# Norm chains at stage changes: work by halves of rows, two ones products a norm, a shared last scaling

## What is computed

```python
def rms_norm(x, w):
    xf = x.astype(jnp.float32)
    y = xf * lax.rsqrt(jnp.mean(xf * xf, axis=-1, keepdims=True) + EPS)
    return (y * w.astype(jnp.float32)).astype(x.dtype)

for layer in range(DEPTH):                       # first block, DEPTH = 2
    mix = mixer(rms_norm(h, norm_pre))
    h = h + rms_norm(mix, norm_post)
    ff = squared_relu_mlp(rms_norm(h, mlp_norm_pre[layer]), mlp_w_up[layer], mlp_w_down[layer])
    h = h + rms_norm(ff, mlp_norm_post[layer])
...
x = x + merged @ w_out[i]                        # second block
x = x + cross_attention(rmsnorm(x, norm_cross[i]), rmsnorm(mem, norm_mem[i]), ...)
x = x + jnp.square(jax.nn.relu(rmsnorm(x, norm_ffn[i]) @ w_up[i])) @ w_down[i]
return rmsnorm(x, norm_final)
```

## Time and profile before

| | |
|---|---|
| median of 3 runs | 2653.78 us (2652.63 to 2654.26) |
| the profiled execution | 2652.97 us, of which the profile's span is 2651.2 us |
| PE busy in the span | 2552.5 us, 96% |
| DVE, ACT, POOL busy | 55%, 44%, 5% |
| PE's share of the chain that ended last | 76% |

### The profile page before, as it was taken

The page is one execution under the profiler, slowest core; times in us unless marked ns, Lnnn a source line. Parts: engine busy times, 40 slices in busy tenths (PEclk is TensorE's granted clock), DMA queues, the critical chain, the costliest instruction groups (busy, mean ns, idle before and its releaser), DMA issues.

```text
span 2651.2 us, 31918 instructions
## 1 busy us (share of the span) xinstructions
PE 2552.5 (96%) x12498; PEld 2076.4 (78%) x12498; DVE 1469.3 (55%) x2349; ACT 1156.8 (44%) x2068; POOL 145.7 (5%) x144
## 2 busy tenths in 40 slices
PE   7999999999999999999989999999999999999998
PEld 5888778878676678888877888878877787788886
DVE  5555454334466654344367888787476566453343
ACT  4254443223356645233246665666245444442232
POOL 1110010000010000000000010000000010000000
PEclk9999999999999999999989999999999999999999
DMA  4212123662232222322323212222321243233222
GB/s 132 72 56 64 61 75 103 125 139 96 80 98 74 79 64 88 103 96 88 103 60 95 63 58 64 64 64 72 104 66 51 71 143 104 72 102 97 96 95 72
DMA packets 188598, 226.00 MB, mean 85 GB/s; under 512 B 8416, under 2 KB 121344, under 8 KB 188192
## 3 DMA queue, kind: packets, MB, share of 16 engines
q1 hardware_dynamic: 188448, 223.95, 28.0%
HBM read 213.96 MB, written 9.44 MB: 84 GB/s over the span
## 4 chain that ended last, share of the span: by engine, by line
PE 76%; DVE 14%; ACT 6%; issue 3%; DMA 2%; POOL 0%; SPq 0%; DVEq 0%; POOLq 0%; ACTq 0%
PE bank L1778 20%; PE bank L1780 20%; PE bank L1779 20%; DVE CV L2473 3%; DVE wlo L2249 2%; PE bank L1784 2%; PE bank L1796 2%; PE bank L1785 2%; PE bank L1786 2%; PE bank L1813 1%; DMA raw<-in_down 1%; DVE E L2522 1%; ACT whi L2032 1%; PE bank L1964 1%; PE bank L1972 1%
## 5 line engine op out<-in xcount | busy, mean ns | idle before, releaser
L2249 DVE TENSOR_TENSOR wlo<-raw,whi 128x1024 fp32r<-128x1024 f32 (+1 forms) x389 | 489.4, 1263 | 719.1 <-ACT whi L2032 717.0
L2032 ACT ACTIVATE whi<-raw 128x1024 fp32r<-128x1024 f32 (+1 forms) x389 | 408.7, 1057 | 647.9 <-PE bank L1780 592.2
L1778 PE MATMUL bank<-XAh,whi 128*128 128x512 f32 x1536 | 615.6, 401 | 19.4 <-DVE XAl L2257 10.9
L1780 PE MATMUL bank<-XAh,wlo 128*128 128x512 f32 x1536 | 602.3, 392 | 0.0
L1779 PE MATMUL bank<-XAl,whi 128*128 128x512 f32 x1536 | 602.2, 392 | 0.0
L1778 PEld LDWEIGHTS bank<-XAh,whi 128*128 128x128 f32 x1536 | 290.7, 189 | 97.8 <-issue 32.2
L1780 PEld LDWEIGHTS bank<-XAh,wlo 128*128 128x128 f32 x1536 | 290.6, 189 | 62.2
L1779 PEld LDWEIGHTS bank<-XAl,whi 128*128 128x128 f32 x1536 | 291.2, 190 | 58.7 <-issue 0.7
L1778 PE MATMUL bank<-XBh,whi 128*128 128x512 f32 x816 | 324.5, 398 | 2.9 <-DVE XBl L2255 1.7
L1780 PE MATMUL bank<-XBh,wlo 128*128 128x512 f32 x816 | 318.0, 390 | 0.0
L1779 PE MATMUL bank<-XBl,whi 128*128 128x512 f32 x816 | 317.9, 390 | 0.0
(11 more groups left out here) (328 smaller groups left out, 3423.4 us busy)
## 6 DMA issues: line engine op xcount, KB each, us to landing
raw<-in_w_in SPq DMA_DIRECT2D x76, 512.0 KB, 3.7
raw<-in_up SPq DMA_DIRECT2D x64, 512.0 KB, 3.5
raw<-in_down SPq DMA_DIRECT2D x64, 512.0 KB, 3.7
raw<-in_a_w_in SPq DMA_DIRECT2D x32, 512.0 KB, 4.0
raw<-in_w_up SPq DMA_DIRECT2D x32, 512.0 KB, 3.6
raw<-in_w_down SPq DMA_DIRECT2D x32, 512.0 KB, 3.6
raw<-in_w_kv SPq DMA_DIRECT2D x16, 512.0 KB, 3.6
raw<-in_w_ssd_branch SPq DMA_DIRECT2D x16, 512.0 KB, 3.4
```

Source lines behind the costliest of these rows:

```text
L1778: pe.matmul(out, wh[:, w, c], xh[:, x, 0:s.ntok], start=st, stop=False)
L1780: m = pe.matmul(out, wl[:, w, c], xh[:, x, 0:s.ntok], start=False, stop=en)
L2032: act.activation(s.hi, s.raw, ACT.Copy).then_inc(s.whi[0], 1)
L2249: dve.tensor_tensor(s.lo, s.raw, s.hi.bitcast(F32), ALU.subtract).then_inc(s.wlo[0], 1)
```

## The change

- `ones` has two products instead of three: tile 6's square is added to the sum too, always on DVE (`left=1`, "sq_add_v"); only tile 7's square is apart.
- Where a norm closes a stage (the four changes and the end), tile 7 leaves its bank in two halves of 256 rows; square, ones products (each half in a bank of its own), logarithm and exponential follow by halves. Tile 0 is scaled, added and split by halves as well.
- Scaling and adding to `h` are two steps now, `res_scale` and `residual`, both on DVE, and the addition of tile k stands behind the split of tile k - 1. (A table could put some additions on POOL; it is empty.)
- The mixers' output products and the last quarter of every `down` product end with tiles 6 and 7 in units of their own.
- While the first tile is prepared, PE gets two products of constants (`WARM`, ones x `cst`), whose result nobody reads.
- A unit that isn't its product's last goes X tile by X tile: all outputs for tile 0, then all for tile 1.
- Behind the second MLP the squares for `norm_mix_2` are taken tile by tile with the splits (`early=True`), and their sums go to POOL instead of DVE.
- At the end ACT multiplies tiles 1 and 4 of `h` by the gain once they are squared; after the factor POOL multiplies these two by `r`, and DVE does the other six.

```diff
-NRAW, NW = 3, 3
+NRAW, NW, WARM = 3, 3, 2
+ADD_ON_POOL = ()
+BY_POOL = 1, 4
...
-            if i < nk - 2:
-                st["added"] = add(by, t=st["sum"], q=q, sq=sq, before=st["added"], n=n, added=sig("sq.add")).added
+            if i < nk - left:
+                st["added"] = add(by if i < nk - 2 else "sq_add_v", t=st["sum"], q=q, sq=sq, before=st["added"], n=n, added=sig("sq.add")).added
...
+            for b, (c0, m) in zip(banks, parts):
+                t = add("ones", q=st["sum"], sq=st["added"], bank=b, c0=c0, n=m, first=True, final=False, ones=sig("ones")).ones
...
+    HALVES = slice(0, 256), slice(256, S)
...
+            if k == 7:
+                es = mix_halves(mx[:, k, :], bk, m, list(mx_free), plus)
+                mt[k] = es[1]
+                bk.free(es[1])
+                tile.halves([mx[:, k, c] for c in HALVES], es)
...
                 if k < 8:
-                    a = add("residual", mx=mx[:, k, :], mix=mt[k], gain=col(g + k), r=r, rfin=rt, h=h[:, k, :], h_ready=ht[k], res=sig("res"))
-                    ht[k] = a.res
+                    sc_ = [add("res_scale", mx=mx[:, k, c], mix=mt[k], gain=col(g + k), r=r.t[:, c], rfin=f, scaled=sig("res.scaled")).scaled
+                           for c, f in (parts if k == 0 else [(ALL, rt[1])])]
                 if k > 0:
                     yield k - 1
+                if k < 8:
+                    halves_of_h[k] = [add("residual_pool" if k in ADD_ON_POOL else "residual", ...).res
+                                      for c, v in zip(HALVES if k == 0 else [ALL], sc_)]
...
+        b = ring_all.take()
         for k in tiles:
+            if k == 0:
+                b.free(add("warm", bank=b, n=WARM, warm=sig("warm")).warm)
             nxt(k)
...
-        p.run(out_gemm_a(6, 2))
+        p.run(out_gemm_a(6, 1))
+        p.run(out_gemm_a(7, 1))
...
-                for hf in range(2):
+                for k0, n in ((0, 4), (4, 4)) if qt < 3 else ((0, 4), (4, 2), (6, 1), (7, 1)):
...
-    nxt, squares, ones = into(XB, "norm_mix_2", "sq_add_v")
+    nxt, squares, ones = into(XB, "norm_mix_2", early=True)
...
+            if s.ends:
+                turns = [(n, o, kk) for n, o in enumerate(s.outs) for kk in range(s.nk)]
+            else:
+                turns = [(n, o, kk) for kk in range(s.nk) for n, o in enumerate(s.outs)]
...
+        elif k == "pre_gain":
+            act.activation(s.h, s.h, ACT.Copy, scale=s.gain).then_inc(s.gained[0], 1)
...
+        if s.kind == "final_pool":
+            pool.tensor_tensor(s.h, s.h, s.r.t[:, :], ALU.mult).then_inc(s.scaled[0], 1)
```

More of the change, by code:

```diff
@@ L446, in rms_close @@
         r = rrs.take()
+        if isinstance(b, list):
+            f = [add("rfin", bank=b[x], ones=m, r=r, c0=x * 256, n=256, dim=dim, rfin=sig("rfin")).rfin for x, m in enumerate(ones)]
+            for x in range(2):
+                b[x].free(f[x])
+            return r, f
         f = add("rfin", bank=b, ones=ones, r=r, n=n, dim=dim, rfin=sig("rfin"))
@@ L487, in rms_steps, with mix_halves @@
         return r, rt
+    HALVES = slice(0, 256), slice(256, S)
+    def mix_halves(mx, bk, m, mx_free, plus):
+        return [add("mix", mx=mx[:, c], bank=bk, cols=c, unit=m, mx_free=mx_free, plus=plus, mix=sig("mix")).mix for c in HALVES]
+    halves_of_h = {}
     def post_norm(mx, g):
@@ L513, in gained, with gained_halves, into @@
         split(X, k, h[:, k, :], ht[k], scale=col(g + k))
-    def into(X, g, by="sq_add"):
-        tile, ones = norm_sum(8, by=by)
+    def gained_halves(X, k, g):
+        for c, v in zip(HALVES, halves_of_h[k]):
+            X.ready[k] = sig("xlo")
+            add("xsplit", hi=X.hi[:, k, c], lo=X.lo[:, k, c], src=h[:, k, c], src_ready=v, src2=NONE, scale=col(g + k), x_free=X.after, xhi=sig("xhi"), xlo=X.ready[k])
+    def into(X, g, by="sq_add", left=1, early=False):
+        tile, ones = norm_sum(8, by=by, left=left)
         def nxt(k):
@@ L521, in nxt @@
                 X.open()
-            gained(X, k, gain[g])
+            (gained_halves if k == 0 and 0 in halves_of_h else gained)(X, k, gain[g])
+            halves_of_h.clear()
+            if early:
+                tile(hsrc(k), ht[k])
         def squares():
             for k in range(8):
-                tile(hsrc(k), ht[k])
+                if not early:
+                    tile(hsrc(k), ht[k])
                 yield
@@ L868, in evac @@
                         yield
[L869 removed]
+                    yield from gemm(us[qt % 2], 8, down, [(k0 * P, n * P)], [("fm", x * P) for x in range(n)], evac, k0=qt * 8, ring=ring_all)
             XB.open()
@@ L1795, in pe_program @@
                 on.room(s.bank)
-            pe.matmul(s.bank.t[:, 0:s.n], K.ones, s.q.t[:, 0:s.n], start=s.first, stop=s.final).then_inc(s.ones[0], 1)
+            c = slice(s.get("c0", 0), s.get("c0", 0) + s.n)
+            pe.matmul(s.bank.t[:, c], K.ones, s.q.t[:, c], start=s.first, stop=s.final).then_inc(s.ones[0], 1)
+        elif k == "warm":
+            on.wait_ge(*K.cst_in)
+            on.room(s.bank)
+            for _ in range(s.n):
+                m = pe.matmul(s.bank.t[:, :], K.ones, K.cst[:, 0:512], start=True, stop=True)
+            m.then_inc(s.warm[0], 1)
         elif k == "hg_diag":
```

128 lines of the change are left out of this document (84 added, 44 removed).

## The result

The changed kernel takes 2645.55 us (median of 8 runs, 2640.93 to 2647.72) where the kernel before takes 2653.89 us on the same chip (8 runs): ratio 0.9967, 95% interval 0.9958 to 0.9976. That is 8.3 us or 0.33% faster, where I had predicted 19.7 us; 2645.5 lies outside my range of 2625 to 2644. Run again beside other kernels it took 2643.65 (4 runs); the median of all twelve is 2645.4.

What follows compares the result with a forecast made beforehand. TensorE, busy 2552.5 of 2651.2 us, was taken as the bound, with idle time, extra norm products and half clock to win. Terms 6.4 + 4.5 + 4.2 + 4.0 + 0.6 = 19.7 us gave 2633.3, 2634 against the median; range 2625 to 2644.

Steps and rivals of the forecast that it cites:

- 1, the chain by halves: At changes one to three, halves of tiles bring PE's first product sooner: 1.7, 3.0 and 1.7 us, 6.4 in all.
- 2, the clock: At changes one to three, shorter idle time keeps PE's clock up more: 1.5 us each, 4.5 in all.
- 12 products of tile 0 give 2.7 us, and DVE's next tile comes 2.05 us later, 2.25 with the new order: At the first change, the order by X tiles removes PE's 0.34 us wait for X tile 1.
- my gap of 2.3 us: Idle time left ahead of PE's first new product; assumed clock loss 1.1 us at each change.
- the change does little: Rival: PE's start is bound by something else, as the next unit's weight split; 2644 to 2652 us, chance 0.07.
- 3, the fourth change: Behind the second MLP, sums on POOL end the ones products at 27.4 instead of 31.6 us: 4.2 gained.
- My variant of that rule: At the fourth change, POOL's sums stop DVE for their whole 1.76 us; this change would gain 0.4 us.
- From there PE is bound by its own products.: Behind the fourth change's ones products, PE's own work is the bound; no gain or loss was forecast there.
- 4, two ones products: In norms inside stages, the memory's and the cross attention's included, one ones product less: together 4.0 us, between 2 and 5.
- 5, the end: Last norm and scaling: factor ready at 3.3 us, DVE's six scalings beside POOL's two take 5.7; 0.6 us gained.
- 6, edits at nothing: Order by X tiles, load shapes and ACT's multiplication by the gain were all to cost no time.
- the rival that ended slower: Order by X tiles makes four-bank gemms wait for banks, up to 2.0 us each; 2665 us at 0.7 each; chance 0.05.

Runs made afterwards that it cites:

- e4: Changed kernel without the two products of constants at the changes; 2645.98 us (5 runs).
- e11: Changed kernel with the units' products bank by bank again, as in the kernel before; 2646.73 us (8 runs).
- The second trace: Changed kernel profiled once more, unedited; 2643.65 us (4 runs).
- e5: Changed kernel with DVE's old order (scale, add, low part) from tile 1 on at the four changes; 2641.83 us (4 runs).
- e7: Changed kernel with three edits: fourth unit's weights split ahead of X tile 5, DVE's old order from tile 1, last scaling on DVE alone; 2639.78 us (4 runs).
- e8: Changed kernel with three ones products again in norms inside stages, the memory's and the cross attention's included; 2648.42 us (10 runs).
- e14: Kernel before with only the order by X tile added; 2654.64 us (10 runs), ratio 0.9999.
- e1: Changed kernel with the fourth unit's weights split ahead of X tile 5 instead of behind X tile 7; 2641.94 us (5 runs).
- e10: e7 with the 96 products of 64 columns in wide form: 24 of 512 columns, a copy, four transposes; 2632.99 us (4 runs).
- e15: Kernel before with only the 64-column products behind the fourth change in e10's wide form; 2648.52 us (8 runs).

## Why the prediction was wrong, point by point

The direction was right, and so was the path of every chain up to its first product. Too high were the terms for the clock, the fourth change and the end, and one loss had no term at all.

**1, the chain by halves: forecast 6.4, right in place.** First products come 6.19, 6.18 and 6.18 us behind the last evacuation's start, 5.9 forecast. From the old stage to the first new product the three changes gain 1.45, 2.65 and 1.45: 5.5 us. A scaling of half a tile takes 0.48 us where the row that I took has 0.425; the logarithm, 0.47, is as in its row.

**2, the clock: forecast 4.5, measured 3.0.** Up to the fourth unit the three changes give 2.2, 4.0 and 3.1 - 0.8 (the norm at 1012) = 2.3, so 8.5 with the path's 5.5 in it. The step that failed is "12 products of tile 0 give 2.7 us, and DVE's next tile comes 2.05 us later, 2.25 with the new order": it compared one tile with one tile. Eight tiles at 2.21 us and the weights behind the last of them end 24.2 us behind the last evacuation, and PE, which had got its speed back, ran into that. I had named the 0.20 us a tile and charged nothing for it. Of what I named as sources, the products of constants bring 1.0 us in all (e4) and the order by X tile up to 4.6 (e11); I had it the other way round.

The idle time of 2.41 us was followed by a fall in one trace and by none in the other, in the same program; my gap of 2.3 us between the rows for 2.59 and 2.39 was right to be undecided. The Trainium skill ("TensorE: Matmul & The Clock Gate", "Why this matters for your kernels") has the full clock kept without a long gap, which would have made the sum 3.3 us better. The second trace speaks against it, with a fall behind 2.41 us; and here the clock at the first change decided nothing: -2.2 us with and without the fall.

The rival *the change does little* (0.07) had named the weight split as the bound. It stood not ahead of PE's first product, as I had it there, but ahead of the fourth unit. That 2645.5 lies in that rival's range is chance, since the first products did come early; and its own figure of 2648 does not follow, as 19.7 - 11 leaves 8.7 us, 2645.

**3, the fourth change: forecast 4.2, measured 1.7.** The price of the contention was nearly right: 1.10 us for each sum (1.0 forecast), tiles 3.31 us apart (3.0 to 3.2). X tile 2 came 12.7 us behind the last evacuation (12.2), but the last tile at 28.7 instead of 26, since each tile also carried the 0.20 us, and one more sum stands on DVE between the last two. And "PE's third unit ends at 24, the ones products at 27.4" left out that the second ones product needs the last tile's square, which is ready only behind that tile's addition and high part: they end at 1356.3, 29.6 us behind the last evacuation. The Trainium skill ("SBUF — State Buffer", "Who interferes with whom") calls the shared ports an exclusive lock; the rows agree, an addition that started 0.18 us after POOL's sum ended 0.55 us after it. My variant of that rule, 0.4 us of gain, took POOL's sum at 1.76 us; it lasts 1.41 here. The measured gain lies between the two.

**Behind it: "From there PE is bound by its own products."** Not wrong, but products have two speeds. I had the trace's stretch of 13.6 us at 1.2 GHz in the profile of before and did not ask what would make it longer. The fall came 1.1 us into the narrow products in the first trace and 4.1 in the second, instead of 6.5 in both traces of before. With what it lasts behind them, that cost 3.2 to 4.9 us, more than the fourth change gained, and with the shortfalls of points 2 and 3 it is most of the miss. Two waits of 0.89 and 0.75 us stand right ahead there, but e5 and e7 have neither and lose the same 3.2 us. That the loss comes with the change is shown; by which part of it is not.

**4, two ones products: forecast 4.0, measured 3.3 by stage and 3.0 by medians (e8).** Right in six norms, the cross attention's loss of 0.3 included. Wrong at 752: I had left 0.45 us of gain there, and the wait of 0.70 us for VectorE's sum takes all of it.

**5, the end: forecast +0.6, measured -0.3.** The factor was ready at 3.4 us (3.3), but two sharers took 6.17 us for DVE's six where I had 5.7, and the last transfers ended 3.7 us behind DVE instead of 3.3. Each POOL product cost DVE (6.17 - 6 x 0.66) / 2 = 1.1 us, as much as each sum above.

**6, edits at nothing.** No wait for a bank and none for a load appeared in PE's list, as forecast, so the rival that ended slower did not come. But the turn order was no nothing (point 2).

**The sum again**, with measured terms: 8.5 at changes one to three, 1.7 at the fourth, 3.3 for the ones products less some 0.3 that came back beside them (against the kernel before, e8's norms at the memory and the cross attention are 0.3 and 0.1 us slower), -0.3 at the end, -3.2 to -4.9 in the 64 columns: 8 to 10 us, where 8.3 were measured. The rest depends on the run: between 1400 and 2100 us the first trace gained 3.1 us more, the second lost 1.6. The range was too narrow because all its cases drew on the same terms; none had a stage behind the change get slower.

**Open.** Why gained time is taken back by the clock in e14 and partly in e11, which part of the change makes the clock fall earlier in the narrow products, and what makes the low stretch there 17, 20.5, 24 or (e1) 31 us long, the runs do not settle. Nor is the wide form's worth in the changed kernel without the three edits known with the copy in its right place.

## What to carry to other kernels

When a wait ahead of a stage is shortened, follow the chain that feeds the stage to its last member, weights included: the first product starts sooner, but the gain is capped where the engine meets the feeding engine's whole queue, and a repair of the clock inside that slack is worth nothing. Count the low clock already in the profile as a cost that the change can enlarge; here it was the largest loss, in a stretch whose instructions the change did not touch, and giving those products another shape (e10, e15) won more than any single edit of the chains. Where VectorE stands while GpSimd works, the two should share work only if VectorE is not the bound, or if what waits for it costs more than 1.1 us an operation.

## What the hardware showed that I had not expected

- TensorE's clock fell inside a run of products of 64 columns with no idle time in it. In both traces of the kernel before, 54 of them ran at 0.111 us each, then the clock fell with PE busy throughout, and the rest took 0.213. In the changed kernel it was 10 and 37, in e5, without a wait in the 13.9 us ahead, about 30. 24 products of 512 columns for the same result took 6.0 us at the full clock.
- The same program, the same idle time of 2.41 us: the granted clock held in one run and fell for 3.4 us in the next. The kernel before showed no such freedom, its falls being the same in two runs.
- A DVE operation that meets a POOL sum waits for the rest of it: 1.78 us instead of 0.68, and 1.1 us again for each POOL product at the end.
